# Prompt attention of a hybrid decoder step: summed outputs turned by transposes and scaled by the scalar engine, queries turned straight from the projection's rows

## The reference

```python
qs = q * (HEAD_DIM ** -0.5)
p_c = masked_softmax(einsum('bqhgd,bchd->bqhgc', qs, kv_cmp[:, :, 0]), m_c)   # compressed
o_c = einsum('bqhgc,bchd->bqhgd', p_c, kv_cmp[:, :, 1])
p_s = masked_softmax(einsum('bqhgd,bqhkd->bqhgk', qs, kv_sel[..., 0, :]), m_s) # selected
o_s = einsum('bqhgk,bqhkd->bqhgd', p_s, kv_sel[..., 1, :])
p_w = masked_softmax(einsum('bqhgd,bkhd->bqhgk', qs, kv_band[:, :, 0]), m_w)   # window of 512
o_w = einsum('bqhgk,bkhd->bqhgd', p_w, kv_band[:, :, 1])
return gates[..., 0:1] * o_c + gates[..., 1:2] * o_s + gates[..., 2:3] * o_w
```

## Time and profile before

| | |
|---|---|
| median of 3 runs (lowest to highest) | 1068.78 us (1066.28 to 1068.86) |
| the profiled execution: its time; its span | 1070.45 us; 1068.7 us |
| PE busy | 953.1 us, 89% |
| DVE busy | 600.2 us, 56% |
| ACT busy | 412.8 us, 39% |
| POOL busy | 202.0 us, 19% |
| mean granted clock of TensorE over the span | 0.94 |

### The profile page before, as it was taken

How to read it: one execution, slowest core, us unless ns; L and a number is a source line. 1 busy time by engine, 2 the same in 40 slices (tenths; PEclk the granted TensorE clock), 3 DMA queues, 4 the chain that set the end, 5 groups by cost and what they waited for, 6 DMA issues and landing times. The chain is left out here.

```text
span 1068.7 us, 16687 instructions
## 1 busy us (share of the span) xinstructions
PE 953.1 (89%) x5935; PEld 819.9 (77%) x5935; DVE 600.2 (56%) x1429; ACT 412.8 (39%) x910; POOL 202.0 (19%) x180
## 2 busy tenths in 40 slices
PE   3999999999799988999899889997888899987887
PEld 2999999999789887877898778774455666765655
DVE  3532010194444676887545677885568566676443
ACT  3532221111224454667244456663534423333312
POOL 3019599999200000000000500000000000000000
PEclk9999999999979999999999889997888889998899
DMA  6226544533232100000110124004343543532311
GB/s 200 90 80 201 196 138 136 161 123 100 69 113 75 41 17 26 1 1 1 41 49 22 44 67 132 1 1 182 87 132 88 152 133 96 164 113 70 96 36 31
DMA packets 106676, 93.73 MB, mean 88 GB/s; under 512 B 21101, under 2 KB 99810, under 8 KB 104482
## 3 DMA queue, kind: packets, MB, share of 16 engines
q1 hardware_dynamic: 84946, 58.65, 18.3%
q10 hardware_dynamic: 19344, 17.25, 5.3%
q0 software_dynamic: 2304, 16.78, 4.5%
HBM read 78.16 MB, written 18.61 MB: 91 GB/s over the span
## 5 line engine op out<-in xcount | busy, mean ns | idle before, releaser
L588 PE MATMUL ps<-w_hi,h_hi 128*128 128x264 f32 (+5 forms) x432 | 124.8, 289 | 0.5 <-DVE h_lo L457 0.5
L588 PE MATMUL ps<-w_lo,h_hi 128*128 128x264 f32 (+5 forms) x432 | 123.6, 286 | 0.0
L588 PE MATMUL ps<-w_hi,h_lo 128*128 128x264 f32 (+5 forms) x432 | 123.5, 286 | 0.0
L1276 DVE TENSOR_TENSOR pt_lo<-ps,pt_hi 128x512 fp32r<-128x512 f32 x132 | 90.9, 689 | 52.3 <-ACT pt_hi L1192 51.6
L1192 ACT ACTIVATE pt_hi<-ps 128x512 fp32r<-128x512 f32 x132 | 78.7, 598 | 83.2 <-PE ps L1099 82.5
L1272 DVE TENSOR_REDUCE least<-ps 128x1 f32<-128x640 f32 (+7 forms) x128 | 90.0, 703 | 13.9 <-PE ps L1088 12.6
L465 DVE TENSOR_TENSOR w_lo<-w_raw,w_hi 128x1024 fp32r<-128x1024 f32 (+2 forms) x12 | 26.9, 2243 | 122.7 <-ACT w_hi L366 122.7
L313 POOL TENSOR_TENSOR chunk<-chunk 128x1024 f32<-128x1024 f32 (+2 forms) x46 | 82.2, 1787 | 3.6
L588 PEld LDWEIGHTS ps<-w_hi,h_hi 128*128 128x128 f32 (+1 forms) x432 | 80.3, 186 | 1.5 <-issue 1.3
L588 PEld LDWEIGHTS ps<-w_lo,h_hi 128*128 128x128 f32 (+1 forms) x432 | 80.4, 186 | 0.0
L588 PEld LDWEIGHTS ps<-w_hi,h_lo 128*128 128x128 f32 (+1 forms) x432 | 80.0, 185 | 0.0
(11 more groups left out here) (379 smaller groups left out, 2294.7 us busy)
## 6 DMA issues: line engine op xcount, KB each, us to landing
kv_pages<-in_cache_slc_kv SPq DMA_DIRECT2D x256, 64.0 KB, 1.9
shared<-in_x_prompt SPq DMA_DIRECT2D x8, 512.0 KB, 3.6
w_raw<-in_w_in SPq DMA_DIRECT2D x8, 512.0 KB
wr_raw<-in_w_in SPq DMA_DIRECT2D x8, 512.0 KB, 4.0
kv_window<-in_cache_win_kv SPq DMA_DIRECT2D x4, 1024.0 KB, 5.4
wo_raw<-in_w_out SPq DMA_DIRECT2D x8, 512.0 KB, 8.4
out<-in_cache_win_kv SPq DMA_DIRECT2D x1, 4032.0 KB
x_row<-in_x_prompt ACTq DMA_DIRECT2D x7, 512.0 KB, 4.8
```

The lines of the kernel that those rows point to most:

```text
L588: mm = nc.tensor.matmul(out, lhs, rhs, start=(k == 0 and i == 0), stop=(k == KD - 1 and i == 2))
L1276: nc.vector.tensor_tensor(pt_lo[:, t % PTS, :], ps[:, turn_bank(t), :], pt_hi[:, t % PTS, :].bitcast(F32), ALU.subtract).then_inc(s_ptl, 1)
```

## The change

1. Output: the product with `ident2` becomes 4 plain transposes of 128 columns. The two halves of each head now stand side by side in bank 7 and are scaled by ACT, one activation for each head (128x128, the factor as a per-partition scale) in a new step `o_scale`; DVE adds twice (the lower half to the accumulator, then the upper). The generator `scaled_later` puts `o_scale` behind the next transposed tile, or ahead of the next use of bank 7, if that comes first.
2. Query: the stage `q_st` goes. PE turns the projection's rows directly (64 columns a head, on partitions 0 to 63 of bank 7), ACT writes `q_hi` twice with the scale in the activation, one for each half of the partitions, and DVE writes `q_lo` on 64 partitions only.
3. Scores: `q_lo` now has 64 rows, so the L1084 and L1063 matmuls with `q_lo` use rows 0 to 63 of `kT` and `kcT` and leave out the product of lo with lo.

```diff
+    def scaled_later(steps):
+        due = None
+        for step in steps:
+            if due and step[0] in ("query", "c_scores", "c_turn", "c_values", "output"):
+                yield due
+                due = None
+            yield step
+            if due and step[0] == "turn":
+                yield due
+                due = None
+            if step[0] == "output":
+                due = "o_scale", step[1], 0
...
-        q_lo = sb("q_lo", [P, 2, NG * P], F32R)
+        q_lo = sb("q_lo", [HD, 2, NG * P], F32R)
...
                     elif what == "query":
-                        pe.wait_ge(s_qst, x + 1)
                         out = spare(("q", x))
                         for g in range(NG):
-                            mm = nc.tensor.transpose(out[:, g * P:(g + 1) * P],
-                                                     q_st[:, g, :, :].rearrange("p a d -> p (a d)"), ident[:, :])
+                            c = (x // NT * NG + g) * HD
+                            mm = nc.tensor.transpose(out[0:HD, g * P:(g + 1) * P],
+                                                     pq[:, x % NT, c:c + HD],
+                                                     ident[:, :])
...
-                            for q in (q_hi, q_lo):
+                            for q, rows in ((q_hi, P), (q_lo, HD)):
                                 mm = nc.tensor.matmul(ps[:, bank, 0:n], q[:, i % 2, y * P:(y + 1) * P],
-                                                      kT[:, br, c * P:c * P + n],
+                                                      kT[0:rows, br, c * P:c * P + n],
...
-                            mm = nc.tensor.matmul(out[:, g * HD:(g + 1) * HD], oT[:, g * P:(g + 1) * P],
-                                                  ident2[:, :], start=True, stop=True)
+                            mm = nc.tensor.transpose(out[:, g * P:(g + 1) * P], oT[:, g * P:(g + 1) * P], ident[:, :])
...
-                        nc.scalar.activation(q_hi[:, x % 2, :], ps[:, 7, :], ACT.Copy).then_inc(s_qhi, 1)
+                        for half in (slice(0, HD), slice(HD, P)):
+                            mm = nc.scalar.activation(q_hi[half, x % 2, :], ps[0:HD, 7, :], ACT.Copy, scale=-SCALE)
+                        mm.then_inc(s_qhi, 1)
...
+                    elif what == "o_scale":
+                        act.wait_ge(s_fac, x + 1)
+                        act.wait_ge(s_sp, place["z", x] + 1)
+                        if x > 0:
+                            act.wait_ge(s_acc, x)
+                        for g in range(NG):
+                            mm = nc.scalar.activation(scaled[:, g, :, :], ps[:, 7, g * P:(g + 1) * P].rearrange(
+                                "p (a d) -> p a d", a=2), ACT.Copy, scale=factor[:, 0, g:g + 1])
+                        mm.then_inc(s_spr, 1)
...
-                        nc.vector.tensor_tensor(q_lo[:, x % 2, :], ps[:, 7, :],
-                                                q_hi[:, x % 2, :].bitcast(F32), ALU.subtract
-                                                ).then_inc(s_spr, 1)
-                        if x + 1 < NKV * NT:
-                            stage_query(x + 1)
+                        nc.vector.scalar_tensor_tensor(q_lo[:, x % 2, :], ps[0:HD, 7, :], -SCALE,
+                                                       q_hi[0:HD, x % 2, :].bitcast(F32), ALU.mult, ALU.subtract
+                                                       ).then_inc(s_spr, 1)
...
-                        nc.vector.tensor_tensor(
-                            scaled[:, :, :], ps[:, 7, 0:NG * HD].rearrange("p (g e) -> p g e", g=NG),
-                            factor[:, 0, :].unsqueeze(2).to_broadcast([P, NG, HD]), ALU.mult
-                        ).then_inc(s_spr, 1)
-                        dve.wait_ge(s_spr, place["z", x] + 1)
+                    elif what == "o_scale":
...
+                        dve.wait_ge(s_spr, place["z", x] + 1)
+                        v.did(nc.vector.tensor_tensor(scaled[:, :, 1, :], acc, scaled[:, :, 1, :], ALU.add))
                         v.wait()
+                        nc.vector.tensor_tensor(out, scaled[:, :, 0, :], scaled[:, :, 1, :], ALU.add).then_inc(s_acc, 1)
+                        dve.wait_ge(s_acc, x + 1)
```

More of the change, by code:

```diff
@@ L739, in schedule @@
         assert not rest
-    steps = list(schedule())
+    def scaled_later(steps):
[10 more added lines that the diff above has]
+                due = "o_scale", step[1], 0
+        if due:
+            yield due
+    steps = list(scaled_later(schedule()))
     at = {s: n for n, s in enumerate(steps)}
@@ L744, in attend_prompt @@
         for kv in range(NKV):
-            assert kv == 0 and i < 2 or at["c_values", kv * NT + i, 0] > at["output", kv * PER_KV + 2 * i - 3, 0]
+            assert kv == 0 and i < 2 or at["c_values", kv * NT + i, 0] > at["o_scale", kv * PER_KV + 2 * i - 3, 0]
             assert i == NT - 1 or at["c_values", kv * NT + i, 0] < at["c_exp", kv * NT + i + 1, 0]
@@ L782, in attend_prompt @@
         stage = sb("stage_b", [P, 2, 364])
-        q_st = sb("q_st", [P, NG, 2, HD])
         kT = sb("kT", [P, 2, SEQ], F32R)
@@ L1286, in _ @@
                         v.wait()
-                        v.did(nc.vector.tensor_tensor(factor[:, 0, :], factor[:, 0, :], gates, ALU.mult))
-                        v.wait()
-                        dve.wait_ge(s_sp, place["z", x] + 1)
-                        nc.vector.tensor_tensor(
-                            scaled[:, :, :], ps[:, 7, 0:NG * HD].rearrange("p (g e) -> p g e", g=NG),
-                            factor[:, 0, :].unsqueeze(2).to_broadcast([P, NG, HD]), ALU.mult
-                        ).then_inc(s_spr, 1)
-                        dve.wait_ge(s_spr, place["z", x] + 1)
+                        nc.vector.tensor_tensor(factor[:, 0, :], factor[:, 0, :], gates, ALU.mult).then_inc(s_fac, 1)
+                    elif what == "o_scale":
+                        kv, i, br = x // PER_KV, x % PER_KV // 2, x % 2
                         acc = o_acc[:, i % 2, :, :]
@@ L1297, in _ @@
                             "p (g d) -> p g d", g=NG)
-                        v.did(nc.vector.tensor_tensor(out, acc, scaled[:, :, :], ALU.add))
+                        dve.wait_ge(s_spr, place["z", x] + 1)
+                        v.did(nc.vector.tensor_tensor(scaled[:, :, 1, :], acc, scaled[:, :, 1, :], ALU.add))
                         v.wait()
+                        nc.vector.tensor_tensor(out, scaled[:, :, 0, :], scaled[:, :, 1, :], ALU.add).then_inc(s_acc, 1)
+                        dve.wait_ge(s_acc, x + 1)
                     elif what == "c_exp":
```

15 lines of the change are left out of this document (3 added, 12 removed).

## The result

| | before | after |
|---|---|---|
| median (runs) | 1068.69 us (4) | 1189.72 us (4) |
| the profiled execution's span | 1068.7 us | 1182.3 us |
| ratio, 95% interval | | 1.1137 [1.107, 1.1203] |
| the prompt's attention | 288 to 730, 442 us | 289 to 850, 561 us |
| what follows it | 339 us | 332 us |

The change makes the kernel 121 us slower. The forecast was 51 us slower, 1120 us, and its range ended at 1145: sign and place were right, the size was not. All of it lies in the prompt's attention. What follows it has the same instructions and is 7 us shorter, at a granted clock of 0.90 where it was 0.88. Of the changed kernels' runs one, of e12 (1096.7 us), fell in a slower state of the device, and medians and ratios leave it out.

What follows compares the result with a forecast made beforehand. PE was taken to bound the prompt's attention, DVE close behind. PE's stream +74 us (88 - 14), waits -23, ACT +6, DVE -2, 4 more off: +51 on 1068.8, 1120 us; range 1072 to 1145, forecast's own 1095 to 1145.

Steps and rivals of the forecast that it cites:

- Bound and place: In the prompt's attention PE sets the pace, DVE close behind; outside this stage no instruction is touched.
- Output on PE, -14: Output: four transposes take 0.36 us against 0.80 for the double-identity product, in 32 units: -14 us of PE's stream.
- Excursions, +88: Scores and compressed branch: 256 switches from 128 rows to 64 and back, 136 x 0.38 + 120 x 0.30 = 88 us.
- eight transposes of 64 columns: Projection's 64-row transposes between L588 matmuls, used to price an excursion: some 0.46 us, going in 0.18, coming out 0.20.
- Rival C: Scores and compressed branch: fp32r ignores the row split, so excursions cost zero; 1063 us, chance 0.12.
- rival D: Attention stage: short pauses bring more stretches at 1.2 GHz, adding 30 us; 1150 to 1180 us, chance 0.04.
- Waits, -23 taken off: PE's visible waits of 34.9 us in the attention's units shrink; two thirds, 23 us, are taken off.
- DVE's -2: Attention: query stage writes go, 9.6 us of DVE; less PE waiting for DVE, counted as 2 us.
- the 4 for waits counted as busy: Sum: 4 us more taken off for waits the records count as busy, an ending matmul's last part.
- ACT's burst, +6: Each unit's four scaling activations delay an exponential PE needs; bounds nothing to 47 us, an eighth taken, 6 us.
- Queries, 0 on PE: Query turn: four transposes stay four, using 64 array columns; taken as 0, or 6 us if columns cost like rows.
- Signs named ahead: Profile after: q_lo ends 0.42 us apart, stage 490 to 500 us, DVE below 65%, ACT 57%, L1133 0.36, tail unchanged.

Runs made afterwards that it cites:

- e12: e10 plus the change's output part as it is (four transposes, ACT scales behind the next turned tile), all products at 128 rows; 1085.7 us, 1.0122 of before.
- e10: Kernel before with the query part alone at 128 rows, q_hi's upper half copied from its lower, so one activation reads bank 7 before q_lo; 1065.4 us, 0.9942.
- e2: Kernel before with the row split alone: q_lo matmuls use rows 0 to 63; 1151.7 us, 1.0793 of before.
- e7: Kernel before with each q_hi product issued three times, all at 128 rows, lengthening PE's stream without pauses; 1121.2 us, 1.0458 of before.
- e4: Kernel before with the change's query part alone, q_hi in two activations, 128 rows in all matmuls; 1077.3 us, 1.0084 of before.
- e13: Kernel before with 64 rows for the 136 wide q_lo products (256 to 512 columns) alone, narrow ones at 128; 1107.6 us, 1.0364 of before.

## Why the prediction was wrong

- **Bound and place: right.** PE sets the pace; only the prompt's attention moved, and what follows it got 7 us shorter.
- **Output on PE, -14: right where it is read.** Four transposes take 0.35 us, as expected (start of the first at 480.50, of what follows at 480.85):

```profile
480.50 0.60 PE L1133 MATMUL ps<-ident,oT 128*128 128x128 f32 x4
480.85 0.48 PE L1097 MATMUL ps<-kT,q_hi 128*128 128x512 f32 x1
```

  In the total little of it shows: PE is busy 397.7 us in e12 against 399.2 in e10. The low clock, 65 us against 44, can take back up to 10 of the 14.

- **Excursions, +88: right in size, nearly, and in mechanism in so far as neighbours with other rows no longer overlap.** The forecast put it that the array empties; the records show the weight load laid bare, and whether the load waits for the array to empty they don't tell. (Its eight transposes of 64 columns come to 0.44 us by its own pace, not 0.46, which makes going in 0.20.) Wide ones cost 0.19 + 0.20 = 0.39 us. Those with 128 columns cost 0.28 (ends at 556.92, 557.16 and 557.43 against 494.83, 494.96 and 495.07 before), those with 16 columns 0.19 (0.20 and 0.21 us a step below, for 0.11 before). The sum is 136 x 0.39 + 56 x 0.28 + 64 x 0.19 = 81 us. Rival C (no price for fp32r) is refuted.

```profile
556.64 0.28 PE L1097 MATMUL ps<-kT,q_hi 128*128 128x128 f32 x1
556.84 0.32 PE L1097 MATMUL ps<-kT,q_lo 64*128 64x128 f32 x1
557.10 0.33 PE L1101 MATMUL ps<-pen_r,ident_r 128*128 128x128 f32 x1
```

```profile
454.44 0.28 PE L1076 MATMUL ps<-kcT,q_hi 128*128 128x16 f32 x1
454.65 0.27 PE L1076 MATMUL ps<-kcT,q_lo 64*128 64x16 f32 x1
454.85 0.28 PE L1076 MATMUL ps<-kcT,q_hi 128*128 128x16 f32 x1
```

- **The sum had no term for the clock: the first of two steps that failed.** The forecast held rival D at 0.04 because "PE never waits long", and priced it at 30 us on top. The pauses are short and many; the low clock rose from 44 to 146 us, of which half, 51 us, is the most that it can cost (idle and waiting time isn't doubled). Taking the other terms off, 119 - (81 - 14 + 13), leaves 39, and the price read from the runs, 0.33 to 0.39 for each of the 102 us, gives 34 to 40. For the row split alone the runs show it: 22 to 36 us (e2 against e7, and e2's own sum).
- **Waits, -23 taken off: the second, and nearly as large.** With ACT's +6, DVE's -2 and the 4 for waits counted as busy, the forecast had waits shorten the time by 23 us in sum. PE's idle time of the change is 13 us more than before, as the output and the queries brought waits of their own: 36 us of the miss. The excursions alone did hide 16 us (e2), so that term was right for them.
- **The miss added up.** The forecast's 51 against the stage's 119 is 68 us: 39 for the clock, 36 for the waits, less the 7 by which the excursions were overpriced. The 39 is what is left over, so the sum closes by construction; only the second reading from the runs is a test of it.
- **ACT's burst, +6: the price was looked for at the wrong place.** The four activations overlap and last 1.13 us together, the lower of the two prices (the forecast took the upper, 1.5), and hardly delay an exponential that PE needs. What they do is hold bank 7, a single buffer with three more users; the forecast did not name who is queued behind `s_spr`. By e12 against e10 the output part costs 20 us where the forecast had -14 + 6 = -8.
- **Queries, 0 on PE: right there, but the chain was missed.** The changed columns cost PE nothing (e4: the four transposes take 0.60 us with 128*64 as with 128*128; PE's new time is waits for q_lo). The query part costs 9 us, and 12 us or more against the form of e10, so the second activation on bank 7 is what costs.
- **DVE: its busy time as forecast in parts.** It is busy 295 us in both. The query part alone takes 5.5 us off (e4, 289.2), the row split alone puts 5.7 on (e2, 300.4). No run shows the -2 on the path by itself.
- **Signs named ahead.** 0.42 and 0.43 us, L1133, DVE below 65% (53%) and, within 7 us, the tail came as said. The stage is 561 us, not 490 to 500, ACT's share 48%, not 57%, and the clock in the stage 0.87, below the 0.9 that was to speak for D. D was no rival of the forecast: it came on top of it, and at 1189.7 us the result lies above D's own 1150 to 1180, since the waits came on top as well.

## What to carry to other kernels

In this kernel a matmul with another number of rows than its neighbours lays its weight load bare, and the next one's (0.39 us for the pair): keep a number of rows throughout a dense stream, even if half of it are zeros, or group the odd ones. Where a change puts many short pauses into such a stream, forecast the clock as a term of the sum, not as an unlikely case, and test it with a kernel that is as long without pauses. Its price can be read from runs that one already has: the same kernel's executions at different mean clocks. Where a consumer is moved to a later step, ask first who else needs the buffer that it empties.

## What was not expected of the hardware

- A change in the number of rows costs the bare weight load, 0.19 to 0.20 us each way, with 512 columns as with fewer (less where the pace before already had part of it: 0.09 to 0.10 at 16 columns). A change in the array's columns costs nothing: the earlier trace rows, and the query transposes with 64 columns (128*64).
- PE at 94% busy (18.75 of 20 us) was granted 0.67 of its clock, and with a gapless stream at 97% (29.06 of 30) 1.00; the kernel before had 1.00 at 87% (17.32 of 20, from 490 to 510 us). The busy share alone doesn't tell the clock, all the more as it counts the bare loads in. The Trainium skill (TensorE: Matmul & The Clock Gate, section A second HAM failure mode: psum-queue depth-cycling) tells of frequent micro-idles that make the clock swing; e2 against e7 agrees with it. What it leaves open stays open here too: the wide excursions alone kept 1.00 in the same stretch of their profiled execution (e13, the row below), and how many pauses of which length it takes was not found.

```profile
430.00:460.00 30.00, 30.00 (x173) 22.34 (x173) 23.52 (x50) 17.88 (x38) 0.00 (x0) 1.00 0.00 1
```

- Whether a second bank for the outputs would turn their transposes into a gain was not tried.
